# Relative-position rows written in 8 DMAs of 3 heads instead of 16 DMAs of 8 rows, and all start-up loads issued by SyncE: a two-layer streaming encoder trunk

## The reference, cut to what matters

```python
for l in range(DEPTH):
    h = rms_norm(x, norm_mix_g[l])
    proj = h @ w_in[l]                      # 1024 x 6400
    lru_x, lru_g, dq, dk, dv, sq, sk, sv = jnp.split(proj, split_at, axis=-1)
    o_lru = rglru_branch(lru_x, lru_g, ...)
    o_diff = diff_attention(dq, dk, dv, lam, ..., bias_diff)   # bias_tab[rel_bucket(k - q)]
    o_swa = swa_attention(sq, sk, sv, swa_sinks[l], bias_swa)
    gates = jax.nn.sigmoid(h @ w_gate[l] + b_gate[l])
    up = jnp.einsum('bsnw,nwd->bsnd', branches, w_branch[l])
    x = x + jnp.sum(gates * up, axis=2) @ w_out[l]
    x = x + peer_ffn(rms_norm(x, norm_ffn_g[l]), ...)          # 128 x 128 product-key experts
return rms_norm(x, final_norm_g)
```

## Time and the profile before

| what | value |
|---|---|
| profiled execution, device time | 2584.68 us |
| its span | 2582.5 us, granted TensorE clock 0.993 |
| median of the runs | 2584.68 us (2582.0 to 2585.07) |
| TensorE busy | 2428.9 us, 94% of the span |
| VectorE, ScalarE, GpSimd busy | 1764.3, 1558.0 and 31.1 us |
| moved by DMA | 413.66 MB, mean 160 GB/s |

### The profile page before, as it was taken

The page is one execution under the profiler, slowest core; times in us unless marked ns, Lnnn a source line. Parts: engine busy times, 40 slices in busy tenths (PEclk is TensorE's granted clock), DMA queues, the critical chain, the costliest instruction groups (busy, mean ns, idle before and its releaser), DMA issues.

```text
span 2582.5 us, 53628 instructions
## 1 busy us (share of the span) xinstructions
PE 2428.9 (94%) x16770; PEld 2237.4 (87%) x16770; DVE 1764.3 (68%) x4132; ACT 1558.0 (60%) x3530; POOL 31.1 (1%) x96
## 2 busy tenths in 40 slices
PE   8998999999999679999999999999999986899998
PEld 8997889999999568888899988899999985688887
DVE  5666764877765986666656667648777659766666
ACT  5567745655555865555555677455555558655555
POOL 0000100000000000000000001000000000000000
PEclk9999999999999999999999999999999999999999
DMA  6554444455554015555544443545555440255554
GB/s 216 190 180 131 133 161 169 163 183 185 184 172 153 0 68 193 194 195 195 194 153 168 168 147 121 174 147 180 186 187 179 167 142 0 96 190 190 191 194 170
DMA packets 116446, 413.66 MB, mean 160 GB/s; under 512 B 8028, under 2 KB 18196, under 8 KB 116116
## 3 DMA queue, kind: packets, MB, share of 16 engines
q1 hardware_dynamic: 115860, 412.44, 46.6%
q10 hardware_dynamic: 512, 0.29, 0.0%
HBM read 411.09 MB, written 4.23 MB: 161 GB/s over the span
## 4 chain that ended last, share of the span: by engine, by line
PE 83%; DVE 9%; ACT 4%; issue 3%; DVEq 1%; DMA 0%; ACTq 0%; POOL 0%; POOLq 0%
PE bank L282 16%; PE bank L284 16%; PE bank L283 16%; PE bank L297 10%; PE bank L298 9%; PE bank L299 9%; DVE hot L1427 3%; DVE w_lo L264 1%; DVE hot L1431 1%; ACT w_hi L251 1%; DVE A L1437 1%; PE bank L374 1%; ACT L324 1%; PE bank L1047 1%; DVEq L1431 1%
## 5 line engine op out<-in xcount | busy, mean ns | idle before, releaser
L264 DVE TENSOR_TENSOR w_lo<-raw,w_hi 128x512 fp32r<-128x512 f32 x1512 | 1028.1, 689 | 744.8 <-ACT w_hi L251 731.8
L251 ACT ACTIVATE w_hi<-raw 128x512 fp32r<-128x512 f32 x1512 | 905.3, 626 | 376.0 <-PE bank L299 310.6
L282 PE MATMUL bank<-h_hi,w_hi 128*128 128x256 f32 x3360 | 963.5, 287 | 14.1 <-DVE w_lo L264 14.0
L283 PE MATMUL bank<-h_lo,w_hi 128*128 128x256 f32 x3360 | 953.8, 284 | 0.0
L284 PE MATMUL bank<-h_hi,w_lo 128*128 128x256 f32 x3360 | 953.7, 284 | 0.0
L282 PEld LDWEIGHTS bank<-h_hi,w_hi 128*128 128x128 f32 x3360 | 647.2, 193 | 23.4 <-DVE w_lo L264 16.6
L283 PEld LDWEIGHTS bank<-h_lo,w_hi 128*128 128x128 f32 x3360 | 647.7, 193 | 0.5
L284 PEld LDWEIGHTS bank<-h_hi,w_lo 128*128 128x128 f32 x3360 | 647.5, 193 | 0.0
L297 PE MATMUL bank<-w_hi,a_hi 128*128 128x512 f32 x1088 | 425.4, 391 | 8.3 <-issue 5.0
L298 PE MATMUL bank<-w_lo,a_hi 128*128 128x512 f32 x1088 | 424.8, 390 | 0.0
L299 PE MATMUL bank<-w_hi,a_lo 128*128 128x512 f32 x1088 | 424.5, 390 | 0.0
(11 more groups left out here) (186 smaller groups left out, 1980.6 us busy)
## 6 DMA issues: line engine op xcount, KB each, us to landing
raw<-stream SPq DMA_DIRECT2D x378, 1024.0 KB, 4.9
hank<-rel_hankel SPq DMA_DIRECT2D x16, 256.0 KB, 2.7
rel_hankel<-rel_line SPq DMA_DIRECT2D x16, 192.0 KB
hank<-rel_hankel SPq DMA_DIRECT2D x16, 128.0 KB, 2.1
A<-subkeys SPq DMA_DIRECT2D x2, 1024.0 KB, 5.0
x<-x_in SPq DMA_DIRECT2D x2, 512.0 KB, 4.2
pr<-lru_w SPq DMA_DIRECT2D x2, 512.0 KB, 8.2
out<-x SPq DMA_DIRECT2D x4, 256.0 KB, 2.0
```

The lines of the kernel that those rows point to most:

```text
L251: act.activation(w_hi[:, (ring % 2) * 2 + k, :], raw[:, slot, sub, 512 * k:512 * k + 512], ACT.Copy).then_inc(w_hi_done, 1)
L264: dve.tensor_tensor(w_lo[:, q, :], raw[:, slot, sub, 512 * k:512 * k + 512], w_hi[:, q, :].bitcast(F32), ALU.subtract).then_inc(w_parts, 1)
L282: pe.matmul(ps, hi, rhs_hi(4 * k + c), start=first, stop=False)
L283: pe.matmul(ps, hi, rhs_lo(4 * k + c), start=False, stop=False)
```

## The change

The four small loads of the start move from ScalarE's queue into SyncE's: `onehot_sb` and `rel_sb` ahead of x, `consts` between x and pair 0, `vecs_sb` between pair 0 and pair 1. VectorE waits for `vecs_sb` as well as `consts` before its first mean square, and ScalarE before it splits block 0; the later waits are dropped. The bias rows are written by 8 DMAs in place of 16, each of all 128 rows of 3 heads (384 KB in place of 192 KB), ahead of the loads of pairs 7 to 14 in place of 4 to 19. The write of the lines moves from behind pair 2 to behind pair 4.

```diff
             def start_sync(sp):
                 sp.sem_inc(w_parts, 8)
+                sp.dma_start(onehot_sb[:], bucket_onehot).then_inc(rel_in, 16)
+                sp.dma_start(rel_sb[:], rel_bias).then_inc(rel_in, 16)
                 for t in range(TT):
                     sp.dma_start(x[:, t, :], x_in[P * t:P * t + P, :]).then_inc(x_in_done[t], 16)
+                sp.dma_start(consts[:], cst).then_inc(const_in, 16)
                 load_pairs(sp, 0, 1)
+                sp.dma_start(vecs_sb[:], vecs.rearrange("l p c -> p l c")).then_inc(vec_in, 16)
                 load_pairs(sp, 1, 2)
-
-            def start_scalar(act):
-                act.dma_start(rel_sb[:], rel_bias).then_inc(rel_in, 16)
-                act.dma_start(onehot_sb[:], bucket_onehot).then_inc(rel_in, 16)
-                act.dma_start(consts[:], cst).then_inc(const_in, 16)
-                act.dma_start(vecs_sb[:], vecs.rearrange("l p c -> p l c")).then_inc(vec_in, 16)
...
-                sp.dma_start(hankel[:, first:first + count, :], bass.AP(tdram.tensor, P - 1 - first, [[N_REL, N_BIAS], [-1, count], [1, SEQ]])).then_inc(hankel_out, 16)
+                sp.dma_start(hankel[first:first + count], bass.AP(tdram.tensor, first * N_REL + P - 1, [[N_REL, count], [-1, P], [1, SEQ]])).then_inc(hankel_out, 16)
...
                 dve.wait_ge(const_in, 16)
+                dve.wait_ge(vec_in, 16)
...
                 if layer == 0:
-                    load_pairs(sp, 2, 3)
+                    load_pairs(sp, 2, 5)
                     rel_line_sync(sp)
-                    load_pairs(sp, 3, 4)
-                    for i in range(16):
-                        rel_rows_sync(sp, 8 * i, 8)
-                        load_pairs(sp, 4 + i, 5 + i)
-                    load_pairs(sp, 20, 26)
-                else:
-                    load_pairs(sp, 2, 26)
+                    load_pairs(sp, 5, 7)
+                    for p in range(7, 15):
+                        rel_rows_sync(sp, 3 * (p - 7), 3)
+                        load_pairs(sp, p, p + 1)
+                load_pairs(sp, 15 if layer == 0 else 2, 26)
                 sp.wait_ge(lru_u.sem, lru_u.base + DC)
-                sp.wait_ge(hankel_out, 16 * 16)
+                sp.wait_ge(hankel_out, 8 * 16)
...
                 norm_squares(act, layer == 0, mix)
                 if layer == 0:
+                    act.wait_ge(vec_in, 16)
                     split_hi(act, 0, 0)
                 split_hi(act, 1, 1)
-                if layer == 0:
-                    act.wait_ge(vec_in, 16)
...
                 split_half(dve, 1, 1, 0)
-                if layer == 0:
-                    dve.wait_ge(vec_in, 16)
                 norm_lo(dve, vec[:, V_MIXG:V_MIXG + DC])
...
                 ch = Chain(act, s_act)
-                start_scalar(act)
```

## The result

The changed kernel takes 2602.89 us, the median of 4 runs (2602.34 to 2605.15), beside 2584.88 us for the kernel before: 18.0 us more, a ratio of 1.0072 with a 95% interval of 1.0056 to 1.0086. The profiled execution took 2601.39 us, with a span of 2599.2 us.

The account below looks back on a forecast made before the run. TensorE, busy in 94% of the span, was taken to bound the kernel. Late weights (15.5 us) plus the later start (2.2) made 17.7 on 2584.68, or 2602.4 us; the forecast's own range was 2594 to 2618, the stated range 2586 to 2616.

Parts of the forecast that it names:

- The number of engines: Bias-row DMAs: the outermost dimension sets the engines sharing a DMA, so 3 engines with 128 rows each, before 12 with 16.
- 128 x 0.047 + 16 x 0.159 us: Work per pair on the three shared engines: 6.02 us of bias rows plus 2.54 us of weights, 8.56 us against 6.61.
- The second rival: Bias-row DMAs: three engines, but others each time, so only the start is lost; 2586.9 us, chance 0.08.
- the fourth rival: SyncE's queue: worse than the upper bound if a full ring also stops its other loads; over 2618 us, chance 0.03.
- How late TensorE comes: Projection, first layer: block 28 can start at 117.2 us in place of 101.7, so TensorE comes 15.5 us late.
- The start: Kernel start: first mean square waits for `vecs_sb`, landing at 9.5 us against 7.33, so TensorE starts 2.2 us later.
- nearly covered: Projection: pair 7, 3 us late, is nearly covered by slack; from pair 8 on every pair makes TensorE wait.
- The clock: TensorE in the projection: waits of some 2 us shouldn't lower its clock; priced at nothing.
- the bound of 4.3: Kernel start, high bound: 4.3 us if `vecs_sb` lands as long after its issue as now, 8.1 us.
- The sum: Whole kernel: 15.5 + 2.2 = 17.7 us more, 2602.4 us; bounds 2593.8 and 2618.1.

Follow-up runs that it names:

- every second pair: Old start, the same 8 DMAs of 3 heads but ahead of every other pair (7, 9, ... 21), against the kernel before: 2589.25 us, ratio 1.0019.

## Why the prediction was right, point by point

**The number of engines.** Right. 28 completions became 19, and 18, 20 and 22 with two, four and six heads, and the plateau follows the number of engines. That each DMA takes the same engines as the last is shown indirectly. The pairs came 8.56 us apart, as worked out from 128 x 0.047 + 16 x 0.159 us for work that adds up on the same engines. And from 81.7 to 83.2 us the next bias rows stood still behind the pair's last share with 13 engines idle. The second rival, other engines each time, would have shown neither. What the windows don't exclude is that something ahead of the engines held the rows back: in the changed kernel SyncE's issue of a pair takes 2.65 to 3.78 us from pair 8 to pair 13, where it took 0.37 us and still takes 0.37 us with six heads. This is a part of what the fourth rival feared; SyncE still stood 110.6 us of the first 160 waiting for free slots, and pair 14 was no later than the engines' work makes it. Which three engines they are, no row names. The rule of the Trainium skill ("DMA: Bandwidth & Descriptors", "Why a DMA increments its semaphore by 16 and not by 1"), the largest number up to 16 that divides the slowest dimension of both sides, agrees with the completions of 24, 6, 4, 3 and 2 heads: 12, 6, 4, 3 and 2. The same section of the Trainium skill says that a DMA from SyncE takes the lowest-numbered engines; that fits the backlog, but no run here shows the numbers.

**How late TensorE comes.** Block 28, the first of pair 14, was to begin 15.5 us late, and later still by the start. In the changed kernel it begins at 120.74 us:

```profile
120.74 0.38 PE bank L282
...
121.59 0.12 PE bank L284
121.71 0.21 PE bank L282
...
124.91 0.21 PE bank L282
125.13 0.12 PE bank L283
...
125.36 0.65 PE bank L1014 x3
```

That is 19.0 us after 101.7. The start's share is read at the end of the first eight blocks, where ScalarE loads its function table, first in the kernel before and then in the changed one:

```profile
38.00 1.28 ACT L324 ACT_TABLE_LOAD   x1
...
41.73 1.28 ACT L324 ACT_TABLE_LOAD   x1
```

3.7 us, which leaves 15.3 us for 15.5. With only the bias rows it is 16.6 - 1.0 = 15.6 us. One detail was wrong: pair 7 was to be nearly covered, and TensorE waited 1.4 us for it. The sum doesn't feel it, because the backlog sets the date of pair 14.

**The clock: the step that failed.** I wrote that the waits shouldn't lower TensorE's clock. They did. In the rows above, the step from one matmul to the next goes from 0.12 to 0.21 us at 121.71 and back at 125.13, and block 28 takes 125.36 - 120.74 = 4.62 us in place of 2.88: 1.7 us lost after a wait of 1.9 us. Windows of the changed kernel:

```profile
core 0: us, PE busy (x) PEld busy (x) DVE busy (x) ACT busy (x) POOL busy (x), PEclk, DMA share, GB/s
65.00:115.00 50.00, 40.75 (x301) 38.93 (x301) 26.68 (x58) 21.91 (x47) 0.00 (x0) 0.97 0.53 173
...
118.00:121.00 3.00, 1.13 (x10) 0.92 (x9) 1.01 (x2) 1.67 (x4) 0.00 (x0) 1.00 0.78 318
121.00:124.00 3.00, 3.00 (x18) 3.00 (x18) 2.73 (x8) 1.51 (x4) 0.00 (x0) 0.60 0.01 3
124.00:127.00 3.00, 3.00 (x20) 2.89 (x19) 1.47 (x3) 1.51 (x4) 0.00 (x0) 0.83 0.22 85
...
127.00:135.00 8.00, 8.00 (x66) 7.89 (x65) 4.18 (x8) 4.21 (x10) 0.00 (x0) 1.00 0.53 182
```

The clock was at its lower level of 1.2 GHz for a few microseconds, after TensorE had been busy 1.13 us of 3.00. The slices of the earlier trace rows from which I argued are 65 us wide and their one digit hides such a stretch. It doesn't follow every wait: of the changed kernel's eight waits two were followed by a low stretch (the other from 70 to 75 us, mean clock 0.66). Nor does it cost time everywhere. With the bias rows alone the clock from 65 to 115 us was 0.90, and in the changed kernel 0.97, yet the splits of pairs 7 to 14 are as far apart: (116.92 - 57.10) / 7 = 8.55 us and 8.56. While late landings set the pace, a slower TensorE only shortens its next wait (with the bias rows alone a wait of 1.82 us, a low stretch, and then one of 0.20 us); what counted was the low stretch after the last late pair, in block 28.

**What came back.** The value stage is 20.8 us late, the second layer 17.2. Of the 3.6 us between, 2.9 lie between two marks of the first layer's end: the table load at 314.43 us and the turning of x at 395.44 are 81.0 us apart before, and 335.35 and 413.46 are 78.1 us apart after. Nothing was changed there. Windows of the kernel before:

```profile
335.00:345.00 10.00, 7.37 (x57) 7.00 (x56) 8.64 (x16) 4.11 (x6) 0.00 (x0) 0.94 0.43 161
345.00:355.00 10.00, 10.00 (x81) 10.00 (x81) 5.15 (x11) 3.83 (x7) 0.00 (x0) 0.89 0.35 109
...
365.00:375.00 10.00, 7.52 (x36) 6.28 (x35) 5.75 (x12) 3.87 (x9) 0.00 (x0) 0.83 0.56 196
```

and the same work of the kernel after:

```profile
335.00:413.00 78.00, 68.71 (x489) 63.49 (x487) 55.88 (x101) 44.22 (x76) 0.46 (x1) 1.00 0.46 162
```

The kernel before has low-clock stretches there, the kernel after has none; in the second layer the same stretch takes 79.8 us in the one (1600.13 to 1679.93) and 79.7 us in the other (1617.19 to 1696.88). So what the forecast lacked at the value stage, 1.7 us of clock and 1.5 us of start, was nearly made good by a later stretch that happened to escape the low clock. That is luck. Why it escaped wasn't tried. In all nine traces the stretch takes 77.8 to 81.8 us; the start alone has 81.4 and the start with the old waits 77.8, so it follows no part of the change. Executions of the kernel before differ as much with nothing changed: of 27, the eight with a granted clock of 0.995 took 2582.0 to 2583.5 us and the two with 0.992 took 2586.6 and 2587.0 us.

**The start.** The direction and the cause were right, the size was low: 3.96 us from trace to trace against 2.2, within the bound of 4.3. The landing of `vecs_sb` at 3.61 + 7.61 = 11.22 us, not 9.5, is the mis-sized term: I had counted bytes at the full rate of a pair, and it landed 7.6 us after its issue, nearly as long as the 8.1 us before, from which the upper bound came. Part of the 3.96 us is the trace I compared with: five runs with the old start have their first mean square at 7.86 to 8.58 us, the profiled one of before at 7.35. The table load at the end of the first eight blocks says the same: 38.00 to 39.61 us in the six traces with the old start, 41.34 and 41.73 in the two with the changed one. By the runs the start costs 3.2 us (1.0 to 5.7 by the interval).

**The sum.** 17.7 us forecast and 18.0 measured, with an interval of 14.5 to 22.2 us. It is a better hit than its terms deserve. At the value stage the traces are 15.3 us for the engines, 3.7 for the start and 1.7 for the clock apart, together 20.7, where the terms were 15.5, 2.2 and nothing. By the end of the profiled executions 16.7 us are left. The two parts alone, 3.2 and 17.2 us, add up to 20.4, with intervals of 1.0 to 5.7 and 14.0 to 20.9 us, so the whole is inside what they allow, and whether the two parts simply add up can't be told to a few microseconds.

## What to carry to other kernels

Before reshaping a DMA, look at its outermost dimension: it decided how many engines shared the copy, and a copy with few outer steps holds its engines for as long as its longest share takes, whatever its bytes. What counts is then the work of the fullest engine in one period of the loads that share it; here it was 8.56 us against 6.61, and every later load was late, while 5.55 us cost nothing. A slack worked out in one stage holds in that stage only: with every second pair, 1.5 us were lost at pair 7 and more in the value stage, and none between. A wait that gathers two landings at the head of an engine's program is as late as the later of them, so give each consumer the wait of its own operand.

## What the runs showed of the hardware

- The throughput of DRAM-to-DRAM rows of 1 KB rose in step with the number of engines, about 47, 70, 95 and 145 GB/s with 2, 3, 4 and 6.
- With 3 engines a pair's packets on the other 13 were through some 4 us before its last share (the fast columns end at about 80.5 us, it landed at 84.43), and SyncE's issue of a pair took up to 3.78 us in place of 0.37.
- TensorE fell to its lower clock for a few microseconds after some of its waits of about 2 us, two of eight in the changed kernel; it cost 1.7 us in one block of 24 matmuls, and the mean granted clock was 0.90 from 65 to 115 us with the bias rows alone changed.
- The same start differs by 1.2 us from run to run (first mean square at 7.35 to 8.58 us in six traces).
